# HGRN2 layers: v and six heads' outputs turned in VectorE's 32x32 blocks and moved by DMA in runs of 512 bytes, the last head's v turned by TensorE

## The reference

```
q, f, v, g = split(rms_norm(x) @ w_in, 4)
q = silu(q);  k = (1 - lb) * sigmoid(-f);  decay = lb + (1 - lb) * sigmoid(f)
per head, token by token (worked in chunks):
    state = decay_t * state + outer(k_t, v_t)
    o_t   = q_t @ state
y = rms_norm(o, per head of 128) * o_norm_w * silu(g)
x = x + y @ w_out
```

## Time and profile before

| | us |
|---|---|
| median of 3 runs | 1346.89 (1344.81 to 1347.1) |
| the profiled execution | 1347.12 |
| its span | 1345.3 |
| granted TensorE clock over the span | 0.999 |

### The profile page before, as it was taken

One profiled execution on the slowest core, in us unless ns is written; L12 is line 12 of the kernel. 1 busy time (PEld: TensorE's weight loads), 2 busy tenths in 40 slices (PEclk: granted clock), 3 DMA queues, 4 the chain that ended last, 5 costly groups with the idle time before them and its releaser, 6 DMA issues.

```text
span 1345.3 us, 22279 instructions
## 1 busy us (share of the span) xinstructions
PE 1334.6 (99%) x8695; PEld 1112.7 (83%) x8695; DVE 929.6 (69%) x1675; ACT 670.5 (50%) x1194; POOL 143.9 (11%) x224
## 2 busy tenths in 40 slices
PE   9999999999999999999999999999999999999999
PEld 8888887888888888888888888788888888888877
DVE  7877788564757576666666686865657577787782
ACT  6444454353655565656565666653534344444450
POOL 2422422000000000000000000000000022332220
PEclk9999999999999999999999999999999999999999
DMA  6433333423222222222223131332333324233421
GB/s 194 107 78 101 79 100 97 127 79 89 68 79 79 79 79 79 79 78 79 79 64 94 47 85 57 99 92 79 94 94 95 110 69 105 71 104 78 111 65 64
DMA packets 248556, 117.86 MB, mean 88 GB/s; under 512 B 40608, under 2 KB 246754, under 8 KB 248451
## 3 DMA queue, kind: packets, MB, share of 16 engines
q1 hardware_dynamic: 248066, 116.23, 31.2%
q0 software_dynamic: 384, 0.20, 0.1%
HBM read 110.10 MB, written 2.10 MB: 83 GB/s over the span
## 4 chain that ended last, share of the span: by engine, by line
PE 92%; DVE 5%; ACT 2%; issue 1%; DMA 0%; SPq 0%; ACTq 0%; DVEq 0%
PE ps L686 38%; PE ps L671 36%; PE scores L686 4%; PE ps L1102 2%; PE ps L1086 2%; PE ps L1042 2%; PE scores L1070 1%; PE ps L1070 1%; DVE w_lo L1786 1%; PE ps L896 1%; PE scores L867 1%; PE ps L700 1%; PE ps L898 1%; PE scores L885 1%; PE ps L1114 1%
## 5 line engine op out<-in xcount | busy, mean ns | idle before, releaser
L671 PE MATMUL ps<-op_hi,w_hi 128*128 128x512 f32 (+1 forms) x800 | 311.4, 389 | 0.1
L671 PE MATMUL ps<-op_lo,w_hi 128*128 128x512 f32 (+1 forms) x800 | 305.2, 382 | 0.0
L671 PE MATMUL ps<-op_hi,w_lo 128*128 128x512 f32 (+1 forms) x800 | 304.8, 381 | 0.0
L686 PE MATMUL ps<-w_hi,op_hi 128*128 128x512 f32 (+1 forms) x728 | 294.9, 405 | 4.9 <-DVE op_lo L1844 4.8
L686 PE MATMUL ps<-w_lo,op_hi 128*128 128x512 f32 (+1 forms) x728 | 283.1, 389 | 0.0
L686 PE MATMUL ps<-w_hi,op_lo 128*128 128x512 f32 (+1 forms) x728 | 282.9, 389 | 0.0
L1786 DVE TENSOR_TENSOR w_lo<-raw,w_hi 128x1024 fp32r<-128x1024 f32 x200 | 244.6, 1249 | 12.6 <-ACT w_hi L1288 11.1
L1288 ACT ACTIVATE w_hi<-raw 128x1024 fp32r<-128x1024 f32 x200 | 202.9, 1052 | 26.5 <-PE ps L686 11.2
L671 PEld LDWEIGHTS ps<-op_lo,w_hi 128*128 128x128 f32 x800 | 150.4, 188 | 29.7
L671 PEld LDWEIGHTS ps<-op_hi,w_hi 128*128 128x128 f32 x800 | 150.6, 188 | 27.7 <-issue 0.3
L671 PEld LDWEIGHTS ps<-op_hi,w_lo 128*128 128x128 f32 x800 | 150.7, 188 | 27.0
(11 more groups left out here) (225 smaller groups left out, 1925.6 us busy)
## 6 DMA issues: line engine op xcount, KB each, us to landing
raw<-in_b_w_in SPq DMA_DIRECT2D x80, 512.0 KB, 3.8
raw<-in_a_w_in SPq DMA_DIRECT2D x64, 512.0 KB, 4.6
raw<-in_c_w_in SPq DMA_DIRECT2D x24, 512.0 KB, 4.3
raw<-in_a_w_out SPq DMA_DIRECT2D x16, 512.0 KB, 4.7
scratch<-scratch SPq DMA_DIRECT2D x256, 16.0 KB, 2.0
raw<-in_b_w_out SPq DMA_DIRECT2D x8, 512.0 KB, 4.0
raw<-in_c_w_out SPq DMA_DIRECT2D x8, 512.0 KB, 4.8
xt<-in_x SPq DMA_DIRECT2D x4, 512.0 KB, 6.4
```

What stands on the lines that cost most here:

```text
L671: last = nc.tensor.matmul(bank, a, b, start=(k == 0 and p == 0), stop=(k == KT - 1 and p == 2))
L686: last = nc.tensor.matmul(bank, a, b, start=(k == 0 and p == 0), stop=(k == KT - 1 and p == 2))
```

## The change

- `move_v`: VectorE's transpose of v writes its blocks in the order window, tile instead of tile, window, so that the 128 columns that go to one window's partitions are contiguous. Each of the 16 transfers of a head is then 32 partitions by one run of 512 bytes. The destination is `a_vq` [partition, quarter of features, tile, 32], and `states` and `values` read v of tile t through `v_tile(t)`, four runs of 32 columns. It is done for the first seven heads of a layer (V_MOVED).
- Last head's v: ScalarE copies the bank to `a_v`, TensorE transposes it at the head of body 8 into `turn[0]`, ScalarE's `v_out` copies that into `a_vq`.
- o of the first six heads (O_MOVED): VectorE's `turn_o` transposes `a_on`'s 32x32 blocks into the space of `a_sq`, SyncE's `move_o` moves them back into the space of `a_on` with 16 transfers of the same form, and `into_y` is four instructions, one per window of 32 tokens of each tile. TensorE's `turn_o` stays in bodies 8 and 9 only. `Square` now waits for `o_landed` before it writes over `a_sq`, and `o_norm` waits for TensorE's transposes only for the last head.

```
@@ -63,6 +63,8 @@
 V_MOVES = 16 * 16
+V_MOVED = HEADS - 1
+O_MOVED = HEADS - 2
@@ -206,11 +208,12 @@
         a_sig, at = carve(at, 3, S)
-        a_vt, at = carve(at, TT, P)
+        a_vq, at = carve(at, 4, TT, WINDOW)
...
         a_st, at = carve(at, 3, P)
-        a_sq, at = carve(at, TT, P)
-        a_on, at = carve(at, TT, P)
+        a_sqf, at = carve(at, S)
+        a_onf, at = carve(at, S)
+        a_sq, a_on = (of.rearrange("p (t c) -> p t c", t=TT) for of in (a_sqf, a_onf))
@@ -323,7 +326,11 @@
         gate_done = sem("gate_done")
+        vT_ready = sem("vT_ready")
+        vT_done = sem("vT_done")
         v_landed = sem("v_landed")
+        o_turned = sem("o_turned")
+        o_landed = sem("o_landed")
@@ -458,6 +465,9 @@
+        def v_tile(t):
+            return a_vq[:, :, t]
+
@@ -526,10 +536,17 @@
                 for q in range(4):
-                    rows = slice(q * WINDOW, (q + 1) * WINDOW)
                     for w in range(WINDOWS):
-                        of = a_v[rows, i % 2].rearrange("a (t w b) -> a w t b", t=TT, w=WINDOWS)[:, w]
-                        sp.dma_start(a_vt[w * WINDOW:(w + 1) * WINDOW, :, rows], of).then_inc(v_landed, 16)
+                        of = a_v[q * WINDOW:(q + 1) * WINDOW, i % 2, w * P:(w + 1) * P]
+                        to = a_vq[w * WINDOW:(w + 1) * WINDOW, q].rearrange("p t b -> p (t b)")
+                        sp.dma_start(to, of).then_inc(v_landed, 16)
+
+            def move_o(idx, i):
+                sp.wait_ge(o_turned, i - 1 + O_MOVED * idx)
+                for w in range(WINDOWS):
+                    for q in range(4):
+                        sp.dma_start(a_onf[q * WINDOW:(q + 1) * WINDOW, w * P:(w + 1) * P],
+                                     a_sqf[w * WINDOW:(w + 1) * WINDOW, q * P:(q + 1) * P]).then_inc(o_landed, 16)
@@ -540,8 +557,10 @@
                             load_columns(IN0[n] + r * 4 + c, w, [part * D + r * P])
-                        if c == 1 and r >= 2:
+                        if c == 1 and 2 <= r < V_MOVED + 2:
                             move_v(idx, r - 2)
+                        if c == 2 and 3 <= r <= HEADS:
+                            move_o(idx, r - 1)
@@ -823,6 +842,13 @@
+                    def turn_v():
+                        pe.wait_ge(v_act, h + 1)
+                        for t in range(TT):
+                            last = nc.tensor.transpose(turn[0][:, t * P:(t + 1) * P],
+                                                       a_v[:, prev, t * P:(t + 1) * P], ident[:])
+                        last.then_inc(vT_ready, 1)
+
@@ -879,10 +905,13 @@
                         pe.wait_ge(kT_done, h + 1)
-                        pe.wait_ge(v_landed, V_MOVES * (h + 1))
+                        if proj:
+                            pe.wait_ge(v_landed, V_MOVES * (i + V_MOVED * idx))
+                        else:
+                            pe.wait_ge(vT_done, idx + 1)
...
                         for t in range(TT - 1):
-                            last = nc.tensor.matmul(score[0][:, t * P:(t + 1) * P], a_kt[:, t], a_vt[:, t],
+                            last = nc.tensor.matmul(score[0][:, t * P:(t + 1) * P], a_kt[:, t], v_tile(t),
@@ -893,7 +922,7 @@
                             to = obank[:, t * P:(t + 1) * P]
-                            last = nc.tensor.matmul(to, a_sd[:, t], a_vt[:, t], start=True, stop=(t == 0))
+                            last = nc.tensor.matmul(to, a_sd[:, t], v_tile(t), start=True, stop=(t == 0))
@@ -963,6 +992,7 @@
                     if mix and not proj:
+                        turn_v()
@@ -989,7 +1019,7 @@
                         steps[17] = [turn_k]
-                        steps[20] = [turn_o, states] if end else [states]
+                        steps[20] = [states]
@@ -1407,6 +1437,13 @@
+                    def v_out():
+                        act.wait_ge(vT_ready, idx + 1)
+                        act.wait_ge(o_ready, h)
+                        nc.scalar.activation(a_vq.rearrange("p q t b -> p t q b"),
+                                             turn[0][:].rearrange("p (t q b) -> p t q b", t=TT, q=4),
+                                             ACT.Copy).then_inc(vT_done, 1)
+
@@ -1444,6 +1481,7 @@
                     if mix and not proj:
+                        v_out()
@@ -1491,11 +1529,16 @@
                     if last_proj:
+                        act.wait_ge(acc_ready, i * 4 + (A0 + 3))
+                        act.wait_ge(v_landed, V_MOVES * (i - 1 + V_MOVED * idx))
+                        nc.scalar.activation(a_v[:, par], acc[0][:], ACT.Copy).then_inc(v_act, 1)
...
                             act.wait_ge(oms_done, h)
+                        if proj and end:
+                            act.wait_ge(o_landed, V_MOVES * (i - 1 + O_MOVED * idx))
@@ -1965,9 +2008,10 @@
                         dve.wait_ge(acc_ready, i * 4 + (A0 + 3))
-                        if i + H0 > 1:
-                            dve.wait_ge(v_landed, V_MOVES * (i + H0 - 1))
-                        nc.vector.transpose(a_v[:, par], acc[0][:]).then_inc(v_act, 1)
+                        if i > 1:
+                            dve.wait_ge(v_landed, V_MOVES * (i - 1 + V_MOVED * idx))
+                        nc.vector.transpose(a_v[:, par].rearrange("p (w t b) -> p t w b", w=WINDOWS, t=TT),
+                                            acc[0][:].rearrange("p (t w b) -> p t w b", t=TT, w=WINDOWS)).then_inc(v_act, 1)
@@ -2075,14 +2119,29 @@
                         dve.wait_ge(rs_done, of + 1)
-                        if not static(of) or of > H0:
-                            dve.wait_ge(oT_ready, of)
+                        if of == H0 + HEADS - 1:
+                            dve.wait_ge(oT_ready, 2 * idx + 1)
...
+                    def turn_o():
+                        dve.wait_ge(on_done, h)
+                        nc.vector.transpose(a_sqf.rearrange("p (q t b) -> p t q b", q=4, t=TT),
+                                            a_on.rearrange("p t (q b) -> p t q b", q=4)).then_inc(o_turned, 1)
+
                     def into_y():
-                        dve.wait_ge(oT_ready, h)
+                        if proj:
+                            dve.wait_ge(o_landed, V_MOVES * (i - 1 + O_MOVED * idx))
+                            for w in range(WINDOWS):
+                                to, gates = (of.rearrange("p (t w a) -> p t w a", t=TT, w=WINDOWS)[:, :, w]
+                                             for of in (y[:, i - 2], a_gate[:, par]))
+                                of = a_onf[:, w * P:(w + 1) * P].rearrange("p (t a) -> p t a", t=TT)
+                                last = nc.vector.scalar_tensor_tensor(to, of, vec[:, 16 + idx:17 + idx], gates,
+                                                                      ALU.mult, ALU.mult)
+                            last.then_inc(y_done, 1)
+                            return
+                        dve.wait_ge(oT_ready, 2 * idx + i - HEADS + 1)
@@ -2133,6 +2192,8 @@
                         split_lo_chunk(IN0[n], len(A_PARTS), j, par, 2, ring)
+                        if end:
+                            turn_o()
@@ -2170,7 +2231,7 @@
                             split_lo_chunk(IN0[n], len(A_PARTS), j if par == 0 else j + 1, 1 - par, c, a_ring)
-                    turn_v()
+                        turn_v()
```

## The result

| | us |
|---|---|
| changed kernel, median of 4 runs | 1358.57 (1356.43 to 1359.29) |
| kernel before, beside it, median of 4 | 1346.99 (1344.81 to 1347.48) |
| ratio, with its 95% interval | 1.0088 (1.0075 to 1.0100) |
| span of the profiled execution | 1357.1 |

The change made the kernel 0.9% slower. 1342.3 us was forecast; what came is rival 1, and dearer than rival 1 was priced. (Medians and ratios here compare executions in which the chip was not disturbed.)

The account below looks back on a forecast made before the run. TensorE's matmuls, 99% of the span, were taken as the bound. 4.4 us on TensorE plus 0.2 on VectorE off 1347.12 gave 1342.5, against the median 1342.3 us; own range 1340.2 to 1344.4, with rival 2 1340.0 to 1346.5.

Parts of the forecast that it names:

- rival 1: SyncE's queue: at an issue pitch of 0.66 us the transfer bursts become the loop; slower, 1350.5 us; chance 0.11.
- the one on SyncE: SyncE's queue: new transfers issue at a pitch of 0.45 us, o lands five microseconds ahead of into_y; cost nothing.
- the ring: SyncE and VectorE, rival 1: move_v, move_o, landing, into_y, splits, turn_v, next move_v take 27.2 us, a body 26.33.
- TensorE's part: Bodies 2 to 6 of both layers: removing turn_o saves 0.44 us each, 4.4 us on the chain.
- Rival 3: TensorE's states and values: runs of 32 columns slow matmuls, 5.2 us against 4.6; no change, 1347.5 us; chance 0.04.
- the stretch at the lower clock: First layer's tail: TensorE at 1.2 GHz for 3.3 us, costing 1.4 us; without any such stretch 1340.9 us.
- Body 7: VectorE there loses turn_v (0.62 us) and gains 0.34 us in into_y; saving counted as 0.1 us a layer.
- Rival 2: Tails of both layers take the gain back (clock, into_y, late v_out): 2.0 us left, 1345 us, no change; chance 0.12.
- The last head's v: Head of body 8: four added TensorE transposes, 0.44 us, use the time turn_o of body 7 left; cost nothing.

Follow-up runs that it names:

- e8: Kernel before with seven bursts of 8 transfers after its end, executed once for issue durations: SBUF to SBUF 0.59 to 0.60 us, 0.42 with DRAM.
- e3: Changed kernel with move_o issuing 8 of its 16 transfers (windows 2 and 3 of o not moved): 1342.15 us, ratio 0.9970.
- e10: Changed kernel with move_o issuing 12 of its 16 transfers (last window of o not moved): 1343.26 us, ratio 0.9974.
- e5: Changed kernel with into_y moved on VectorE from ahead of the two splits and turn_v to behind next_queries(0): 1341.45 us, ratio 0.9963.
- e6: Changed kernel with each burst of 16 transfers, for v and o, replaced by five through DRAM: 1342.25 us, ratio 0.9969.
- e9: e5 with only five heads' o by VectorE and transfers; body 7 keeps TensorE's transposes and one-instruction into_y at its old place: 1338.84 us, ratio 0.9943.
- e1: Changed kernel with v's part alone: VectorE's turn_o, move_o and four-part into_y taken out, TensorE turns o everywhere: 1343.42 us, ratio 0.9978.

## Why the prediction was wrong

**The step that failed is the one on SyncE**: "I bound them by 0.33 and 0.60 us and take 0.40, a pitch of 0.45 us, nearer the plain rows." It measured 0.591, a pitch of 0.63 us, and some 0.68 on average over a burst, in which the odd issue takes up to 1.7 us. The nearest row was that of the very transfer being changed (L532), and I set it aside because both patterns became plain. e8 shows that the pattern was never the price: what L532 shares with the new transfers, both sides in SBUF, is what costs. The bound of 0.60 was right; the choice inside it, a pitch of 0.45, lay on the wrong side of the 0.63 us from which rival 1 closes its ring. With it fell what was built on it: o was to have landed five microseconds ahead of into_y, and into_y waited for it in all 12 bodies, 44.1 us in all.

**Rival 1 was right in its mechanism.** e3 and e10 show that the loss hangs on the number of issues, with a threshold between 28 and 32 a body; e5 shows that it needs the ring, since 32 issues cost nothing once into_y stands behind turn_v; e6 breaks it from the other side. **Its price was too small**, 1350.5 against 1358.6. Most of the 8.1 us is the turn: 28.0 us in place of 27.2 makes 0.8 x 5 = 4 us a layer. The start of into_y in body 7 bears that out. Beside the kernel before, and counted from each layer's first block of scores, it is 5.5 us late in the first layer (224.19 against 218.44) and 5.2 in the last (1294.65 against 1284.50); rival 1 had it 4.1 - 2.2 = 1.9 late in each. That is 6.9 of the 8.1 us. The turn is longer by the odd long issues, by a load that takes 0.58 us between bursts in place of 0.37, and in body 2 by an into_y of 1.7 us; I read this off the traces and took none of it away in a run. Behind into_y are the remaining 1.2 us: the load on the last layer's chain, and the lower clock level, at 4.0 us against about 1.4, less what the tail saves elsewhere. The four executions point the same way, 1356.43 us at a granted clock of 0.999 and 1358.28 to 1359.29 at 0.996 or 0.997. No run has the ring without the late load or the longer stretches, so these two are not separated further.

**The Trainium skill's rule** ("DMA: Bandwidth & Descriptors", Anatomy of one DMA) is stated for GpSimd's path, and these transfers go by SyncE's queue; here too fewer runs hardly shortened an issue (591 against 601 ns, and e8's L598 against L606). It spoke for rival 1, and a chance of 0.11 was too little.

**TensorE's part was right.** With the ring open the scores follow each other at 26.33 us in bodies 2 to 7 (e3, e10; 26.32 in e9), 0.44 us less than before. Rival 3 is out: matmuls on runs of 32 columns are in those 26.33 us. **That e3, e5 and e6 stand at 1341.5 to 1342.3, beside the forecast of 1342.3, is in part luck.** The forecast kept the stretch at the lower clock, and most of their executions (13 of 17) don't have it; the forecast's own figure without one was 1340.9, where e3 and e6 stand at 1342.1 and e5 at 1341.3.

**Body 7 was wrong in its terms, and in its sum by a little.** 0.1 us a layer was to be won there. In the last layer, where neither kernel has a stretch at the lower clock, the way from body 7's scores to states of body 8 takes 34.67 us in e3 against 34.33 before: 0.3 lost. e9 against e5 shows that o's part in body 7 as a whole, the transposes taken from TensorE and the four into_y together, costs 2.6 us in the two layers; giving it up is faster. The four into_y take 1.13 to 1.14 us in bodies 3 to 6 (1.0 forecast), but 1.84 (e5) and 1.90 in body 7, where GpSimd works beside them, and 1.71 in the changed kernel's body 2, where it does so too; that GpSimd is the cause is argued from this overlap, not tested. That o's part takes back what v's part won in the tail is what e1 against e3 shows: 1.6 us of waits in the tails against 4.8.

**Rival 2's sum has a slip.** It takes 0.6 us a layer where its terms, 0.65 and 0.2, make 0.85: 1345.4 us and not 1345. Nothing hangs on it.

**The last head's v** cost nothing that shows, as forecast: e1 has it whole, and is faster. What it costs by itself no run says.

## What to carry to other kernels

When a change adds transfers to a queue, add up the ring: from the release of a burst through its landing, its reader and whatever stands in order behind the reader, back to the release. If that is longer than the loop it lies in, the kernel runs at the ring's pace whatever its busiest engine does; and the cheapest cure can be to move the reader behind the instruction that releases the next burst (one call, 17 us). And price an operation by the row of its own kind before rows that only look alike.

## What the runs showed of the hardware

- An issue on SyncE from SBUF to SBUF takes 0.59 to 0.60 us, whatever the partitions, bytes and runs tried (e8); now and then one in a burst takes longer, up to 1.8 (L532, L542). With one side in DRAM it takes 0.42 to 0.43 in a burst and 0.32 to 0.37 alone (e8), but a weight load right behind a burst of SBUF-to-SBUF issues took 0.58 (changed kernel, L517 at 157.04).
- 256 KB through DRAM in five transfers keep SyncE for 6.4 us (e6); the same in 16 transfers between partitions, for 10.0 to 11.9 (changed kernel).
- Around the end of a 3.2 us wait of TensorE its clock was at the lower level for 3.4 and 6.8 us. After waits of 1.2 us (e1, e9) no such stretch is seen in the tails. After waits of up to 1.5 to 1.7 us it came in one tail of the profiled execution (the first layer's in the earlier trace rows, the last layer's in e10) or in none (e3, e5, e6). The same kernel ran with and without it, 1.4 us apart (1346.9 and 1345.5, e1's neighbours).
